# A static schedule for the first mixer, with one undivided gate chunk in every attention unit

## The reference

```python
proj = xn @ w_in                                   # qa, ka, va, fa, cq, ckv, kr, ga, gb
log_f = log_sigmoid(fa + b_forget)
ya = forgetting_attention(qa, ka, va, log_f)       # 8 heads of 64, bias = difference of cumulated log_f
qb = rms_norm(cq, q_a_norm_g) @ w_q_up             # 8 heads of 64 + 32 rotated
kv = rms_norm(ckv, kv_a_norm_g) @ w_kv_up
yb = latent_attention(qb, rope(qb), k_nope, rope(kr), v)   # 8 heads, mask by chunks of 64
gate_a, gate_b = sigmoid(ga + b_gate[:D]), sigmoid(gb + b_gate[D:])
merged = gate_a * (ya @ w_branch_a) + gate_b * (yb @ w_branch_b)
h = x + merged @ w_out
```

## Time and profile before

| what | value |
|---|---|
| median of 3 runs | 2401.26 us |
| the profiled execution: time, span | 2401.09 us, 2399.3 us |
| PE busy | 2258.1 us (94%) |
| mean granted TensorE clock | 0.958 |
| v's third chunk to the first transpose | 50.5 us |
| first attention, first transpose to last value product | 88.2 us |
| up projections and first scores of the second attention | 46.4 us |
| second attention | 126.4 us |
| merge, until the output product begins | 61.9 us |

### The profile page before, as it was taken

One profiled execution on the slowest core, in us unless ns is written; L12 is line 12 of the kernel. 1 busy time (PEld: TensorE's weight loads), 2 busy tenths in 40 slices (PEclk: granted clock), 3 DMA queues, 4 the chain that ended last, 5 costly groups with the idle time before them and its releaser, 6 DMA issues.

```text
span 2399.3 us, 29972 instructions
## 1 busy us (share of the span) xinstructions
PE 2258.1 (94%) x10380; PEld 1857.4 (77%) x10380; DVE 1161.6 (48%) x1941; ACT 894.7 (37%) x1528; POOL 429.3 (18%) x355
## 2 busy tenths in 40 slices
PE   5988699899999999999997999999999799999997
PEld 4766588678888888888885888888887678888886
DVE  4344644445444235444236766676657534544423
ACT  3223455433223133222213345565654443322212
POOL 1021111212111004221003620020035232111100
PEclk8976899999999999999997999999999999999999
DMA  3200122123333323333322512212243433333331
GB/s 125 88 18 0 38 62 71 61 88 99 94 101 92 107 86 97 96 96 96 105 88 93 157 58 67 62 62 75 67 154 119 146 125 90 98 94 98 104 97 68
DMA packets 63795, 212.35 MB, mean 89 GB/s; under 512 B 7168, under 2 KB 7424, under 8 KB 63328
## 3 DMA queue, kind: packets, MB, share of 16 engines
q1 hardware_dynamic: 50832, 182.08, 24.5%
q10 hardware_dynamic: 10272, 20.98, 2.5%
q0 software_dynamic: 2608, 8.19, 1.1%
HBM read 196.02 MB, written 14.68 MB: 88 GB/s over the span
## 4 chain that ended last, share of the span: by engine, by line
PE 82%; DVE 7%; ACT 4%; POOL 3%; issue 2%; DMA 2%; ACTq 0%; DVEq 0%; POOLq 0%; SPq 0%; PEldq 0%
PE bank L178 26%; PE bank L180 25%; PE bank L179 25%; PE bank L1711 1%; ACT w_hi L147 1%; DVE w_lo L152 1%; POOL hid L538 1%; DMA w_raw<-stream 1%; PE bank L235 1%; DVE gn_r L2254 1%; DVE xg L246 1%; PE bank L662 1%; PE bank L653 0%; DVE xn_lo L461 0%; DVE norm_r L240 0%
## 5 line engine op out<-in xcount | busy, mean ns | idle before, releaser
L152 DVE TENSOR_TENSOR w_lo<-w_raw,w_hi 128x1024 fp32r<-128x1024 f32 x337 | 460.0, 1368 | 642.5 <-ACT w_hi L147 642.2
L178 PE MATMUL bank<-xn_hi,w_hi 128*128 128x512 f32 x1656 | 660.8, 399 | 34.4 <-DVEq L916 17.8
L180 PE MATMUL bank<-xn_hi,w_lo 128*128 128x512 f32 x1656 | 651.0, 393 | 0.0
L179 PE MATMUL bank<-xn_lo,w_hi 128*128 128x512 f32 x1656 | 650.6, 393 | 0.0
L147 ACT ACTIVATE w_hi<-w_raw 128x1024 fp32r<-128x1024 f32 x337 | 353.2, 1052 | 398.8 <-PE bank L180 261.2
L178 PEld LDWEIGHTS bank<-xn_hi,w_hi 128*128 128x128 f32 x1656 | 314.1, 190 | 105.7 <-issue 29.9
L180 PEld LDWEIGHTS bank<-xn_hi,w_lo 128*128 128x128 f32 x1656 | 313.9, 190 | 66.8
L179 PEld LDWEIGHTS bank<-xn_lo,w_hi 128*128 128x128 f32 x1656 | 314.5, 190 | 62.7 <-issue 0.7
L178 PE MATMUL bank<-h_hi,w_hi 128*128 (+1 forms) x528 | 205.9, 390 | 4.1 <-DVE hid L482 3.7
L180 PE MATMUL bank<-h_hi,w_lo 128*128 (+1 forms) x528 | 205.5, 389 | 0.0
L179 PE MATMUL bank<-h_lo,w_hi 128*128 (+1 forms) x528 | 205.4, 389 | 0.0
(11 more groups left out here) (390 smaller groups left out, 3325.7 us busy)
## 6 DMA issues: line engine op xcount, KB each, us to landing
w_raw<-stream SPq DMA_DIRECT2D x337, 512.0 KB, 3.5
x<-xt SPq DMA_DIRECT2D x2, 1024.0 KB, 6.0
spill_x<-x ACTq DMA_DIRECT2D x1, 2048.0 KB, 6.6
spill_ga<-ga_out ACTq DMA_DIRECT2D x8, 256.0 KB, 2.0
spill_rv_hi<-rv_hi_out ACTq DMA_DIRECT2D x8, 256.0 KB, 2.6
spill_rv_lo<-rv_lo_out ACTq DMA_DIRECT2D x8, 256.0 KB, 4.9
spill_gr<-gr_out ACTq DMA_DIRECT2D x8, 256.0 KB, 4.3
decay<-decays POOLq DMA_DIRECT2D x8, 256.0 KB, 3.0
```

Source lines behind the costliest of these rows:

```text
L152: nc.vector.tensor_tensor(w_lo[:, slot, :], w_raw[:, slot % 2, :], w_hi[:, slot, :], ALU.subtract).then_inc(split_lo, 1)
L178: nc.tensor.matmul(to, a_hi, b_hi, start=start, stop=False, skip_group_check=True)
L179: nc.tensor.matmul(to, a_hi, b_lo, start=False, stop=False, skip_group_check=True)
L180: return nc.tensor.matmul(to, a_lo, b_hi, start=False, stop=stop, skip_group_check=True)
```

## The change: what it does

The loops of the first mixer are written out, and its work is put in another order.

- The 16 gate chunks are shared out: 8 in the first attention (`b1_ga`, before the up projections in the stream) and 8 in the second (`b1_gb`). Every unit (one head) does transposes 1 and 2, one whole gate chunk, transposes 3 and 4, the scores of the head after next, then its value products.
- DVE evicts the gate chunk to `gate_out`, a pair of buffers in x's place, and ACT sends it to DRAM (`spill_g1`, 256 KB for each chunk). DVE's order in a unit is: biases of the next head's scores, low parts, scaling of the next head, low part of a weight chunk, eviction. ACT waits for that eviction before it goes on with the next unit.
- The latents' norms no longer stop the v projection. Their reciprocals stand in units 1 and 2 of the first attention on DVE, the rest in units 3 to 5. The rotation is made during the projections. ACT instead of DVE copies the cumulated gates, and they are read in place, without POOL's copy.
- In the up projections, q, k and v come in another order, so that the first scores stand between them. DVE rotates q while it evicts it.
- Splits of y go into units 4 to 7 of the second attention. The merge makes its first two tiles by halves (first branch first) over eight banks. Gates come back from DRAM by POOL's DMAs in two pairs of buffers (the first two pairs in unit 6), sigmoids are made tile by tile, and x is loaded again from the input by 8 DMAs of ACT.
- The second mixer keeps its work; it takes over two semaphores and counts on from the first.

```diff
 STAGES = [
-    ("b1_qk", 8), ("b1_c", 3), ("b1_fk", 1), ("b1_v", 4), ("b1_up", 4),
-    ("b1_gates", 16), ("b1_merge", 8), ("b1_out", 8), ("f0_in", 2 * FT), ("f0_down", FT),
+    ("b1_qk", 8), ("b1_c", 3), ("b1_fk", 1), ("b1_v", 4),
+    ("b1_ga", 8), ("b1_up", 4), ("b1_gb", 8), ("b1_merge", 8), ("b1_out", 8), ("f0_in", 2 * FT), ("f0_down", FT),
     ("f1_in", 2 * FT), ("f1_down", FT),
...
+        gate_out = sb("gate_out", [P, 2, S], F32, 40 * K)
+        g1_saved = sem("saved_g1")
+        g1_d = nc.dram_tensor("spill_g1", (16, P, S), F32, kind="Internal").ap()
...
+            def units_pe(pe):
+                def turn(h, kb):
+                    at_least(pe, s["lo"], 4 * h + kb - 1, z["lo"])
+                    for qb in range(kb, TB):
+                        if kb == 0:
+                            pe.wait_ge(s["scaled"], 4 * h + qb + 1 + z["scaled"])
+                        last = nc.tensor.transpose(banks[4 + kb % 2][:, (qb - kb) * P:(qb - kb + 1) * P],
+                                                   prob[:, h % 2, OFF[qb] + kb * P:OFF[qb] + (kb + 1) * P], ident[:])
+                    last.then_inc(s["turned"], 1)
+
+                def values(h, kb):
+                    if kb == 0:
+                        at_least(pe, s["out"], h - 1, z["out"])
+                        pe.wait_ge(s["v_lo"], h // 2 + 1 + z["v_lo"])
+                    pe.wait_ge(s["lo"], 4 * h + kb + 1 + z["lo"])
+                    at = slice(KOFF[kb], KOFF[kb + 1])
+                    mm3(banks[6 + h % 2][:, kb * P:S], vs_hi[:, kb, :], vs_lo[:, kb, :], pt_hi[:, at], pt_lo[:, at],
+                        kb == 0, kb == TB - 1).then_inc(s["summed"], 1)
+
+                def fill(slot, tiles):
+                    for k in tiles:
+                        w = slice(k * P, (k + 1) * P)
+                        last = mm3(banks[3][:], w_hi[:, slot, w], w_lo[:, slot, w], xn_hi[:, k, :], xn_lo[:, k, :],
+                                   k == 0, k == KT - 1)
+                    return last
+
+                for h in range(HEADS1):
+                    turn(h, 0)
+                    turn(h, 1)
+                    slot = ready(pe, fg, h)
+                    at_least(pe, s["cleared"], h, z["cleared"])
+                    fill(slot, range(KT)).then_inc(used, 1)
+                    turn(h, 2)
+                    turn(h, 3)
+                    if h + 2 < HEADS1:
+                        score(pe, h + 2)
+                    for kb in range(TB):
+                        values(h, kb)
...
+            def units_act(act, between):
+                def highs(h, blocks):
+                    for kb in blocks:
+                        act.wait_ge(s["turned"], 4 * h + kb + 1 + z["turned"])
+                        at_least(act, s["summed"], 4 * (h - 1) + kb + 1, z["summed"])
+                        nc.scalar.activation(pt_hi[:, KOFF[kb]:KOFF[kb + 1]], banks[4 + kb % 2][:, 0:S - kb * P],
+                                             ACT.Copy).then_inc(s["hi"], 1)
+
+                for h in range(HEADS1):
+                    highs(h, (0, 1))
+                    if latent and h + 2 < HEADS1:
+                        stage(act, h + 2)
+                    if h:
+                        output(act, h - 1)
+                    if h and h % 2 == 0:
+                        stage_v(act, h // 2)
+                    if h + 1 < HEADS1:
+                        exps(act, h + 1, (0, 1, 2))
+                    highs(h, (2, 3))
+                    if h + 1 < HEADS1:
+                        exps(act, h + 1, (3,))
+                    if not latent and h % 2 == 0 and h + 2 < HEADS1:
+                        stage(act, h + 2)
+                    ahead(high_part, act, fg, h)
+                    between(act, h)
+                    act.wait_ge(s["cleared"], h + 1 + z["cleared"])
+                    act.dma_start(g1_d[gate0 + h], gate_out[:, h % 2, :]).then_inc(g1_saved, 16)
+                output(act, HEADS1 - 1)
...
+            def units_dve(dve, between):
+                for h in range(HEADS1):
+                    if h + 1 < HEADS1:
+                        biased(dve, h + 1)
+                    for kb in range(TB):
+                        dve.wait_ge(s["hi"], 4 * h + kb + 1 + z["hi"])
+                        at = slice(KOFF[kb], KOFF[kb + 1])
+                        nc.vector.tensor_tensor(pt_lo[:, at], banks[4 + kb % 2][:, 0:S - kb * P], pt_hi[:, at],
+                                                ALU.subtract).then_inc(s["lo"], 1)
+                    if h + 1 < HEADS1:
+                        scaled(dve, h + 1)
+                    ahead(low_part, dve, fg, h)
+                    finished(dve, fg, h)
+                    at_least(dve, g1_saved, 16 * (gate0 + h))
+                    apart(dve)
+                    nc.vector.tensor_copy(gate_out[:, h % 2, :], banks[3][:]).then_inc(s["cleared"], 1)
+                    between(dve, h)
+
+            def units_pool(pool, between):
+                for h in range(HEADS1):
+                    if h + 2 < HEADS1 and (latent or h % 2 == 0):
+                        stage_low(pool, h + 2)
+                    if h and h % 2 == 0:
+                        stage_v_low(pool, h // 2)
+                    between(pool, h)
...
+                    if j == 2:
+                        pe.wait_ge(m["squared"], b["squared"] + 3)
+                        for k in range(3):
+                            last = nc.tensor.matmul(banks[1 + k // 2][:], ones[:], c_sq[:, k, :], start=k != 1, stop=k != 0)
+                            if k:
+                                last.then_inc(m["summed"], 1)
+                        pe.wait_ge(a["lft_lo"], 1)
+                        pe.wait_ge(a["fk"], 1)
+                        cumulated(0)
+                        cumulated(1)
+                pe.wait_ge(m["root"], b["root"] + 2)
...
+                pe.wait_ge(m["root"], b["root"] + 2)
+                pe.wait_ge(a["negc"], 1)
+                pe.wait_ge(s["mask"], 2)
+                a_score(pe, 0)
+                pe.wait_ge(a["negc"], 2)
+                cumulated(2)
+                for h in range(3, 7):
+                    pe.wait_ge(a["v"], h - 2)
+                    cumulated(h)
+                pe.wait_ge(a["negc"], 3)
+                cumulated(7)
+                a_score(pe, 1)
+                pe.wait_ge(a["negc"], 8)
+                a_pe(pe)
+
+
+                for j in range(4):
+                    slot = ready(pe, fu, (0, 1, 2, 3)[j])
+                    if j == 0:
+                        pe.wait_ge(m["lo"], b["lo"] + 3)
+                        pe.wait_ge(s["biased"], 32 + az["biased"])
+                        pe.wait_ge(s["cleared"], 8 + az["cleared"])
+                    if j in (0, 3):
...
+                    if j == 1:
+                        for n in range(8):
+                            if n == 0:
+                                pe.wait_ge(s["lo"], 32 + az["lo"])
+                                pe.wait_ge(s["out"], 7 + az["out"])
+                            elif n == 3:
+                                pe.wait_ge(s["out"], 8 + az["out"])
+                            elif n >= 4:
+                                pe.wait_ge(a["mq"], n - 3)
...
+                        pe.wait_ge(a["mk"], 7)
+                        pe.wait_ge(a["rope"], ROPE_PARTS)
+                        b_score(pe, 0)
+                b_score(pe, 1)
+                pe.wait_ge(a["mv"], 4)
+                pe.wait_ge(a["mq"], 8)
+                b_pe(pe)
...
+                def between_a(dve, h):
+                    if h in (1, 2):
+                        dve.wait_ge(m["root"], b["root"] + h)
+                        nc.vector.reciprocal(c_r[:, h - 1, :], c_r[:, h - 1, :]).then_inc(m["recip"], 1)
+                    if h == 3:
+                        dve.wait_ge(m["recip"], b["recip"] + 2)
+                        for k in range(3):
+                            nc.vector.scalar_tensor_tensor(y1[:, 4 + k, :], y1[:, 4 + k, :], col[:, C_GAINS[k]:C_GAINS[k] + 1],
+                                                           c_r[:, k // 2, :], ALU.mult, ALU.mult).then_inc(m["scaled"], 1)
...
+                def between_b(pool, h):
+                    for k in ({4: (0, 1), 5: (2, 3), 6: (4, 5), 7: (6,)}.get(h, ())):
+                        lows_of_y(pool, k)
+                    if h == 6:
+                        pool.wait_ge(g1_saved, 16 * 8)
+                        gates_to(pool, 0)
+                        gates_to(pool, 1)
...
+                def half(T, slot, g):
+                    for k in range(4):
+                        pe.wait_ge(s["y_lo"], 4 * g + k + 1)
+                        w = slice((4 * g + k) * P, (4 * g + k + 1) * P)
+                        last = mm3(banks[2 * (T % 4) + g][:], w_hi[:, slot, w], w_lo[:, slot, w], y1_hi[:, 4 * g + k, :],
+                                   y1_lo[:, 4 * g + k, :], k == 0, k == 3)
+                    return last
+
+                slots = []
```

(94 more changed lines are left out.)

851 lines of the change are left out of this document (326 added, 525 removed).

## The result

The changed kernel takes 2336.6 us (median of 4 runs, 2335.3 to 2339.0), the kernel before 2400.2 us in the same comparison. The ratio is 0.974, 95% interval 0.972 to 0.975: 64 us faster. The forecast was 2318 us, the range 2300 to 2350.

What follows compares the result with a forecast made beforehand. PE bounds the second attention; in the first it waits for other engines and works slowly; the ring bounds the merge. Terms -17.5 + 7.0 - 20.0 - 43.4 - 8.9 = -82.8 us gave 2318 us, range 2300 to 2350.

Steps and rivals of the forecast that it cites:

- start: Before the first attention: 31.9 us of PE work plus 1.1 us of waits, 33.0 us for 50.5, saved 17.5.
- up projections: Between the attentions: 23.1 us of PE work, 1.3 for the gate eviction, 2.0 of latencies: 26.4 us, saved 20.0.
- Second attention: Units of 10.71 us, two without scores 8.8, plus 1.1 at unit 6: 83.0 us for 126.4, saved 43.4.
- rival (a): Both attentions: round trip about 12.2 us, so ACT sets the unit; +24 us in 16 units, 2342 us; chance 0.12.
- Do the other engines keep up: Both attentions: ACT 6.9, DVE 7.8 us per unit, round trip 9.7 us under units of 10.71 and 12.36; PE stays bound.
- The clock: New attention units: full clock assumed, from second-mixer units with one chunk beside a head at 1.00.
- rival (d): First attention: clock stays at the low level, PE's time doubles, +91.8 us, 2410 us; chance 0.03.
- The reciprocals in units 1 and 2: First attention: two DVE reciprocals of 3.4 us delay transposes 3, all but some 1.7 us each covered; 3.4 us for both.
- The first attention as a whole: Six units of 12.36 and two of 8.8 us make 91.8, plus 3.4 for reciprocals: 95.2 us, 7.0 more than before.
- Merge: Bound by the ring ACT, DVE, POOL, ACT; low parts at 10, 17, then every 6.0 us: 53.0 us, saved 8.9.
- (b): First attention: the gate chunks hide nothing, +37.1 us, 2355 us; chance 0.07.
- (c): Merge: gate spill and reload make sigmoids late in each pair of tiles, some 3 x 4 us, 2330 us; chance 0.04.

Runs made afterwards that it cites:

- early staging: Changed kernel with the next heads' staging in the first attention moved ahead of the last exponentials, as in the second attention: 2314.9 us, ratio 0.964.
- the kernel with both edits: Changed kernel with staging moved earlier in the first attention and the gate chunk cut in two halves in both attentions: 2307.8 us, ratio 0.962.
- early staging and full height: Changed kernel with staging moved earlier in the first attention, whose scores read all 128 rows instead of 64: 2297.1 us, ratio 0.958.
- x was spread: Against the kernel with both edits, one x load behind each tile's sigmoids in the merge instead of eight at its head: 2305.6 us, ratio 0.961.

## Why the prediction was right, and where it was not

The time lies in the range because the range was wide and one stage alone missed. That 7.6 us came from stages without a term is luck.

*What bounds the kernel; start; up projections.* Right. The start took 31.2 us with PE busy in all of it: my 1.1 us of waits did not appear, 31.9 us of work was 31.2. The up projections took 25.6 for 26.4, with one wait of 1.7 us for the gate's eviction where I had put 1.3, and 0.6 us of other idle time where I had put 2.0. At clock 1.00 both (0.78 and 0.82 in the earlier trace rows).

*Second attention.* Right: 82.9 for 83.0, units 10.65 us for 10.71. PE is the bound, but by a hair, as the margin of 1.0 us said: halving the chunk gives 2.2 us.

*The price of rival (a)* was wrong. A round trip of 12.2 us adds 1.5 us to units of 10.71, but nothing to the six units of 12.36. With the second attention alone it is 8 x 1.5, so about 2330 us and not 2342.

*Do the other engines keep up.* This is the step that failed, for the first attention. I made one round trip for both stages and counted "staging and output 1.6" on ACT ahead of the exponentials. In the diff that holds for the second attention only. In the first, the staging is issued behind the last exponential, so that POOL's two low parts (2 x 1.3 us) are not beside the exponentials but between them and the scores. The round trip there is not 9.7 us: behind the last transposes come ACT's last exponential, 0.53 us of a high part and 2.7 us of POOL, and PE stands for 4.5 us, in three units. Symptom (a) of my list ("PE idle before each score for ACT or POOL") was the one that showed, in one stage, from a queue position and not from latencies. Moving the staging took 20 us off, and the mirror image in the other stage put 39.5 us on: shown.

*The clock.* The term for it was zero, and rival (d) had 0.03. It came true in part, and its sign, rows at 0.50 inside the units, was there. I read 1.00 in units with one chunk beside a head, and the timeline shows 128 rows in every matmul of such a unit; the half-height scores stood in the same prediction as a reason for (d), and I gave them 1.65 us of length, none of clock. With no gap they leave the clock at 0.90, an estimated 9 to 10 us lost; with the gaps it was 0.83. A check of the size: the stage with early staging, less this loss, is 91.3 to 92.5 us. My sum without the reciprocals was 91.8, with no wait at the end, where 1.2 us stood. The two units at 1.00 in the kernel with both edits took 12.2 us, where I had 12.36.

*The reciprocals in units 1 and 2.* They took 3.34 us each on DVE as reckoned, but no wait of PE follows them: the term of 3.4 us measured 0. In the kernel with early staging and full height, whose units are shorter, one wait of 0.5 us for a low part appeared.

*The first attention as a whole:* 91.8 + 13.5 (three gaps) + 1.2 (eviction at its end) + 16.4 = 122.9; the 16.4 is what is left for the low clock, and was not measured by itself. The mean clock of 0.83 puts some 42 us of the stage at half speed, part of it inside the gaps, so 21 us is the most it can have cost.

*Merge.* 53.6 for 53.0. It holds by luck, by terms that cancel. The third and fourth low parts were ready 12.2 and 19.4 us after the last value product; the 10 and 17 us of my sum had no row behind them. The loads at the head took 3.76 us instead of 2.6. The ring then turned in 5.68 us instead of 6.0, which gave back 1.9 of these 2.4 us. The output product waited for the tenth low part, as the sum had it, with PE idle for 5.6 us ahead of it. Timelines of the changed kernel, ACT's queue and DVE, which answer to the earlier trace rows:

```profile
380.17 3.76 ACTq L1269 DMA_DIRECT2D x<-xt  x8
```

```profile
392.14 1.47 DVE L152 TENSOR_TENSOR w_lo<-w_raw,w_hi 128x1024 fp32r<-128x1024 f32 x1 [3.08 <-ACT w_hi L147]
...
397.82 1.48 DVE L152 TENSOR_TENSOR w_lo<-w_raw,w_hi 128x1024 fp32r<-128x1024 f32 x1 [3.02 <-ACT w_hi L147]
```

*Rivals (b) and (c)* did not come: the chunks hid in the first attention what they were to hide, and no wait of the merge is put down to a gate load (after x was spread, one of 1.3 us on ACT appeared, and cost nothing).

*The rest.* 7.6 us less outside the first mixer had no place in the sum. Unchanged instructions ran at a somewhat higher clock there, the low stretches of about 3 to 10 us lying elsewhere and differing between kernels that change nothing in them. Why is open; no run was made for it. In the changed kernel's other profile (span 2336.5 us) the output product starts at 430.6 us, which leaves 1905.9 us behind it: the size repeats.

## What to carry to other kernels

When one helper serves two stages through a branch, read the branch for each stage and write down the queue position of every instruction in it: three lines of ACT's order cost 20 us here and would have cost 39 in the other stage. Price a wait with the clock behind it, which here made 4.5 us into 6.5 to 7.1. And price the clock per stage from rows with the same shapes of matmuls: a row at 1.00 from units of another shape was weak evidence. Last, read an edit in the trace of its own stage as well as in the median: splitting a tile sooner took 5.4 us off the merge while the medians stood 2.0 apart.

## What the runs showed of the hardware that was not expected

**Half-height matmuls are dearer at full clock too.** The first score group of a head on the timeline of PE, changed kernel (64 rows), then the kernel with full height:

```profile
170.62 0.32 PE L178 MATMUL bank<-ks_hi,qs_hi 64*128 64x128 f32 x1
170.78 0.27 PE L179 MATMUL bank<-ks_lo,qs_hi 64*128 64x128 f32 x1
170.89 0.27 PE L180 MATMUL bank<-ks_hi,qs_lo 64*128 64x128 f32 x1
171.09 0.33 PE L660 MATMUL bank<-tri_r,ident_r 128*128 128x128 f32 x1
171.35 0.44 PE L178 MATMUL bank<-ks_hi,qs_hi 64*128 64x384 f32 x1
```

```profile
147.05 0.31 PE L178 MATMUL bank<-ks_hi,qs_hi 128*128 128x128 f32 x1
147.19 0.28 PE L179 MATMUL bank<-ks_lo,qs_hi 128*128 128x128 f32 x1
147.30 0.28 PE L180 MATMUL bank<-ks_hi,qs_lo 128*128 128x128 f32 x1
147.41 0.27 PE L660 MATMUL bank<-tri_r,ident_r 128*128 128x128 f32 x1
147.53 0.39 PE L178 MATMUL bank<-ks_hi,qs_hi 128*128 128x384 f32 x1
```

From one group's start to the next it is 0.73 against 0.48 us. The third matmul follows the second at the same distance in both (0.11 us); the mask's 128-row matmul follows a 64-row one after 0.20 instead of 0.11, and the next 64-row one after 0.26 instead of 0.12. So the change of height costs, 1.18 us for the eight changes in a head's scores (3.57 against 2.39 us), about 0.15 each with what they delay. The Trainium skill ("TensorE: Matmul & The Clock Gate", Why this matters for your kernels) says that a single matmul on 32 rows takes the time of one on 128 rows. Where matmuls on 64 rows follow each other, the 0.11 us agrees; in a mix of heights the time is longer. Why such scores also lower the clock in an engine that is never idle, the runs don't tell.

**A scaling on DVE beside POOL's low parts took 3.30 us instead of 1.28.** The same four operations in two units of the changed kernel:

```profile
150.92 3.30 DVE L797 TENSOR_SCALAR prob<-prob,small 128x128 f32<-128x128 f32 x4
...
172.11 1.28 DVE L797 TENSOR_SCALAR prob<-prob,small 128x128 f32<-128x128 f32 x4
```

POOL's two low parts run from 151.27 to 153.94 us beside the first, and nothing runs on POOL beside the second. The Trainium skill ("GPSIMD Engine Reference", 8. Key points) says that POOL shares its SBUF interfaces with DVE, with contention when DVE works in a 2-port mode or reads two SBUF inputs. That agrees, though no row shows which of the two holds for this operation. The runs on the place of the staging, made for another question, bear the link out. With early staging the low parts lie elsewhere, and each scaling in the first attention's units takes 1.27 or 1.28 us. With late staging in both, the six scalings of the second attention that lie beside low parts take 3.36 or 3.37 us, where the changed kernel has 1.27. The first of them:

```profile
301.01 3.36 DVE L795 TENSOR_SCALAR prob<-prob,small 128x128 f32<-128x128 f32 x4
```
